# Encoder layer with a mixture of experts: the routing chain rewritten, the closing sums and scaling in halves and on three engines, the fifth weight tile issued behind the first row gather

## The reference

```python
x = x + y @ w_out
h = rmsnorm(x, ffn_norm)
# group top-1 of 4, then expert top-2 of the 8 in that group
lg = h @ w_group + b_group;  grp = argmax(lg);  p_grp = softmax(lg)[grp]
le = (h @ w_router + b_router)[grp];  top_p, top_i = top_k(softmax(le), 2)
gate = p_grp * top_p / sum(top_p);  expert = grp * 8 + top_i
# for each token and each of its two experts (w_gate, w_up 2048x768, w_down 768x2048)
x += gate * ((silu(h @ w_gate[e]) * (h @ w_up[e])) @ w_down[e])
return rmsnorm(x, final_norm)
```

## Time and profile before

| | |
|---|---|
| median of 3 runs | 2051.66 us (2050.88 to 2051.67) |
| the profiled execution | 2052.39 us, span 2050.5 us |
| TensorE busy | 1879.7 us, 92% of the span |
| VectorE busy | 584.6 us, 29% |
| ScalarE, GpSimd busy | 174.1 us, 241.6 us |
| moved by DMA | 681.13 MB, mean 332 GB/s |

### The profile page before, as it was taken

One profiled execution on the slowest core, in us unless ns is written; L12 is line 12 of the kernel. 1 busy time (PEld: TensorE's weight loads), 2 busy tenths in 40 slices (PEclk: granted clock), 3 DMA queues, 4 the chain that ended last, 5 costly groups with the idle time before them and its releaser, 6 DMA issues.

```text
span 2050.5 us, 21069 instructions
## 1 busy us (share of the span) xinstructions
PE 1879.7 (92%) x9592; PEld 1072.9 (52%) x9592; DVE 584.6 (29%) x789; ACT 174.1 (8%) x248; POOL 241.6 (12%) x92
## 2 busy tenths in 40 slices
PE   8999999999949999999988989998898999889895
PEld 6887878788834444344444434444443444434342
DVE  3221656611141222221222222122222222222224
ACT  4000110100110000100000010000001000000102
POOL 3323444433300000000000000000000000000000
PEclk9999999999969999999999999999999999999998
DMA  7222132443269999999999999999999999999993
GB/s 271 82 78 82 62 103 87 164 176 114 105 271 389 432 431 429 429 429 429 431 427 430 430 430 430 429 430 428 429 430 429 429 431 427 432 429 428 430 429 136
DMA packets 67131, 681.13 MB, mean 332 GB/s; under 512 B 10272, under 2 KB 13536, under 8 KB 40288
## 3 DMA queue, kind: packets, MB, share of 16 engines
q1 hardware_dynamic: 63632, 670.11, 78.4%
q0 software_dynamic: 2304, 8.39, 1.0%
q10 hardware_dynamic: 1104, 1.25, 0.2%
HBM read 679.73 MB, written 8.39 MB: 336 GB/s over the span
## 4 chain that ended last, share of the span: by engine, by line
PE 58%; DMA 38%; DVE 3%; POOL 0%; issue 0%; ACT 0%; SPq 0%; DVEq 0%; POOLq 0%
DMA region_rest<-in_w_gate 23%; PE banks L982 21%; PE banks L690 14%; PE banks L871 9%; DMA region_h<-in_w_gate 6%; DMA region_w<-in_w_gate 6%; PE banks L1001 5%; PE banks L973 4%; DMA region_rest<-in_w_down 2%; PE banks L960 1%; PE banks L949 1%; PE banks L908 1%; PE banks L755 1%; PE banks L767 1%; DMA region_h<-x_rows,region_rest 1%; DVE region_rest L1196 0%
## 5 line engine op out<-in xcount | busy, mean ns | idle before, releaser
L982 PE MATMUL banks<-region_rest,region_w 128*64 128x384 f32 x2432 | 411.5, 492 | 49.9 <-DMA region_rest<-in_w_gate 33.3
L982 PEld LDWEIGHTS banks<-region_rest,region_w 128*64 128x64 f32 x2432 | 175.9, 138 | 277.1 <-issue 199.0
L1428 DVE TENSOR_TENSOR region_x<-banks,region_x 128x1024 f32<-128x1024 f32 x128 | 150.8, 1219 | 585.7 <-PE banks L973 585.7
L690 PE MATMUL banks<-split_h,split_w 128*128 128x512 f32 x896 | 286.0, 396 | 3.6 <-POOL split_w L437 3.1
L1001 PE MATMUL banks<-region_rest,region_w 128*64 128x512 f32 x936 | 232.9, 655 | 19.5 <-DVE region_w L1453 13.0
L437 POOL TENSOR_TENSOR split_w<-region_rest,split_w 128x2048 fp32r<-128x2048 f32 x43 | 201.4, 4684 | 319.5 <-DVE split_w L1086 319.5
L690 PEld LDWEIGHTS banks<-split_h,split_w 128*128 128x128 f32 x896 | 169.0, 189 | 40.2 <-issue 4.9
L690 PE MATMUL banks<-split_w 128*128 128x512 f32 x448 | 175.0, 391 | 0.0
L483 POOL DMA_INDIRECT region_h<-x_rows,region_rest x16 | 16.0, 1000 | 1281.1 <-PE banks L960 1263.5
L871 PE MATMUL banks<-split_w,split_h 128*128 128x512 f32 x512 | 160.1, 394 | 0.0
L982 PE MATMUL banks<-region_h,region_w 128*64 128x384 f32 x832 | 142.9, 497 | 17.4 <-DMA region_h<-in_w_gate 10.1
(11 more groups left out here) (196 smaller groups left out, 1159.2 us busy)
## 6 DMA issues: line engine op xcount, KB each, us to landing
region_rest<-in_w_gate SPq DMA_DIRECT2D x40, 3072.0 KB, 31.6
region_rest<-in_w_down SPq DMA_DIRECT2D x39, 3072.0 KB, 31.0
region_rest<-in_w_up SPq DMA_DIRECT2D x36, 3072.0 KB, 29.9
region_h<-in_w_up SPq DMA_DIRECT2D x14, 3072.0 KB, 30.0
region_w<-in_w_up SPq DMA_DIRECT2D x14, 3072.0 KB, 29.4
region_w<-in_w_down SPq DMA_DIRECT2D x13, 3072.0 KB, 31.1
region_h<-in_w_gate SPq DMA_DIRECT2D x12, 3072.0 KB, 31.1
region_w<-in_w_gate SPq DMA_DIRECT2D x12, 3072.0 KB, 31.1
```

Source lines behind the costliest of these rows:

```text
L690: mm = t_.matmul(ps[:, 4 * (c % 2) + m, :], w[s][:, kk, cols_m], h[:, k, :], start=(k == 0 and w is w_hi and h is h_hi), stop=(k == KT - 1 ...
L982: mm = t_.matmul(ps[h * SLOTS:(h + 1) * SLOTS, u, 0:HF], hTe[:, k, :], ring_gu[slot][:, kk, h * HF:(h + 1) * HF], start=(k == 0), stop=(k ...
L1428: v.tensor_tensor(tile, ps[:, 2 + 2 * c:4 + 2 * c, :], tile, ALU.add).then_inc(comb_added, 1)
```

## The change

- **Routing.** The logits are no longer multiplied by 1/rms. In its place the bias is multiplied by rms and added before the last part of the logits arrives; the exponentials take 1/rms as their scale, one for each of 4 blocks. The sum over earlier blocks and the base of each expert's slots come out of TensorE (4 products in place of 1 for the rank, one of them issued before the routing is known; 4 small ones for the counts behind them). VectorE makes the slots in 4 operations; `compare` for the first pair comes in two halves of 512 columns, and `plan` starts on the first half. The overflow slots are made later, behind `read_plan`.
- **Rows into `hTe`.** Transposes are signalled after 8 and after 16, `store_rows_T` takes two operations of 512 columns, parts 0 and 1 wait for a half each.
- **Tile 4** waits for the first gather too (`rows_gathered`).
- **Last tile** (part 5 of the last expert) is issued as 3 DMAs of a third each, `down` waits for each third.
- **End.** `combine` for c = 0 waits only for the first half of the low parts. VectorE scales columns 0 to 1407; for the other 640 POOL multiplies by `final_norm` into `gained`, and ScalarE, behind its last root, by 1/rms. The output of t waits for both.
- One small constant (`e64_next`) is made by POOL in the first stage.

```diff
@@ sync
             sp.wait_ge(x2_sq, 4 * NT)
+            sp.wait_ge(rows_gathered, 16)
             tile(4)
...
-                tile(n)
+                if n == TILES - 1:
+                    for k in range(DK):
+                        sp.dma_start(ring_down[slot_of(n)][:, k:k + 1, :], wdn_v[E - 1, 1][:, k:k + 1, :])\
+                            .then_inc(last_landed[k], 16)
+                else:
+                    tile(n)
...
                 sp.wait_ge(out_ready, t + 1)
+                sp.wait_ge(out_rest_ready, t + 1)
@@ gpsimd
+            pool.wait_ge(final_landed, 16)
+            for t in range(NT):
+                pool.wait_ge(comb_added, 4 * E - 6 + 2 * t)
+                g.tensor_tensor(gained[:, t, :], x_sb[:, t, FINAL:], final_row[:, FINAL:], ALU.mult).then_inc(f_gained, 1)
@@ scalar
+            ae.wait_ge(x2_rms, 3)
             ae.wait_ge(exp_in, 1)
-            a.activation(lgm, lgm, ACT.Exp).then_inc(exp_out, 1)
+            for t in range(NT):
+                a.activation(lgm[:, t, :], lgm[:, t, :], ACT.Exp, scale=stat[:, 20 + t:21 + t]).then_inc(exp_out, 1)
...
+            for t in range(NT):
+                ae.wait_ge(f_gained, t + 1)
+                ae.wait_ge(f_rinv, t + 1)
+                a.activation(x_sb[:, t, FINAL:], gained[:, t, :], ACT.Copy, scale=stat[:, 8 + t:9 + t]).then_inc(out_rest_ready, 1)
@@ tensor
+            t_.matmul(by_tile, ones[0:1, :], e64[0:1, :]..., start=True, stop=False)
             pe.wait_ge(routed, 1)
-            t_.matmul(ps[:, 0, 0:NT * E], before, A..., start=True, stop=True)
-            t_.matmul(ps[:, 1, 0:NT * E], ones, A..., start=True, stop=True).then_inc(counted, 1)
+            for n in range(1, NT):
+                t_.matmul(ps[:, 6, n * E:NT * E], ones, flat[:, 0:(NT - n) * E], start=False, stop=False)
+            t_.matmul(ps[:, 6, 0:NT * E], before, flat, start=False, stop=True).then_inc(counted, 1)
+            for t in range(NT):
+                mm = t_.matmul(ps[:, 7, 0:E], ones, A[:, t, :], start=(t == 0), stop=(t == NT - 1))
+            mm.then_inc(counted, 1)
...
                 if t == 0:
-                    pe.wait_ge(m_lo_ready, i * 4 + 4)
                     pe.wait_ge(back_ready, i * 2 + 2)
                 for c in (0, 1):
+                    if t == 0:
+                        pe.wait_ge(m_lo_ready, i * 4 + (3 + c))
...
-                pe.wait_ge(hte_ready, e + 1)
                 for part in range(4):
+                    if part < 2:
+                        pe.wait_ge(hte_ready, 2 * e + part + 1)
@@ vector
-                v.scalar_tensor_tensor(x_sb[:, t, :], x_sb[:, t, :], stat[:, 8 + t:9 + t], final_row,
+                v.scalar_tensor_tensor(x_sb[:, t, 0:FINAL], x_sb[:, t, 0:FINAL], stat[:, 8 + t:9 + t], final_row[:, 0:FINAL],
```

More of the change, by code:

```diff
@@ L57 @@
 NOBODY = 4096
+FAR = 8192.0
 UK = 4
@@ L244, in build @@
         tile_landed = [sem(f"tile_landed{s}") for s in range(RING + 1)]
+        last_landed = [sem(f"last_landed{k}") for k in range(DK)]
         over_landed = [sem(f"over_landed{s}") for s in range(PARTS)]
@@ L993, in transpose_act, with down @@
                 pe.wait_ge(at_ready, e + 1)
-            def down(b, part, slot):
+            def down(b, part, slot, pieces=None):
                 q = part - 4
                 for kk in range(DK):
+                    if pieces:
+                        pe.wait_ge(pieces[kk], 16)
                     for n in (0, 1):
@@ L1009, in landed @@
                 return s
-            plan(0)
+            plan(0, True)
             pe.wait_ge(plan_read, 9)
@@ L1032, in _ @@
                     pe.wait_ge(m_lo_ready, 2 * e)
-                for part in (4, 5):
-                    down(b, part, landed(n + part))
+                down(b, 4, landed(n + 4))
+                if e < E - 1:
+                    down(b, 5, landed(n + 5))
+                else:
+                    down(b, 5, slot_of(n + 5), last_landed)
             for t in range(NT):
@@ new lines, in _, with per_choice @@
+            next_first = e64_next.rearrange("p (a b) -> p a b", a=1).to_broadcast([P, NT, E])
+            then(v.tensor_tensor(t1, rank, next_first, ALU.is_ge))
+            then(v.scalar_tensor_tensor(Q, t1, FAR, rank, ALU.mult, ALU.add))
+            def per_choice(of):
+                return of.rearrange("p (k a) b -> p k a b", k=1).to_broadcast([P, 2, NT, E])
+            then(v.tensor_tensor(both, full, per_choice(Q), ALU.mult))
+            then(v.tensor_reduce(slot.rearrange("p a k -> p k a"), both, AX.X, ALU.add))
@@ L1400, in next_compare, with compare @@
+            def compare(first, last, ready, order=0):
+                n = last - first
+                v.tensor_tensor(pick[:, first:last], row_slot[order].rearrange("p (a b) -> p a b", a=1).to_broadcast([P, n, P]),
+                                slot.rearrange("p a (b c) -> p (a b) c", c=1)[:, first:last].to_broadcast([P, n, P]),
+                                ALU.is_equal).then_inc(ready, 1)
             def next_compare(i, order=0):
@@ L1404, in next_compare @@
                 ve.wait_ge(slots_shifted, i)
-                compare(order)
+                compare(0, NA, pick_ready, order)
             def read_plan(i, s):
```

114 lines of the change are left out of this document (64 added, 50 removed).

## The result

The changed kernel takes 2039.97 us (median of 4 runs, 2038.62 to 2043.66), the kernel before took 2051.27 us beside it (4 runs, 2050.46 to 2051.67): ratio 0.9941, interval 0.9929 to 0.9953. It is faster; the forecast was 2040.0.

The account below looks back on a forecast made before the run. The weight stream through DMA was taken to set the loop's pace, leaving its start and its end. 8.8 us at the start and 3.05 at the end, 11.85, gave 2040 us for the median; range for 8 in 10, 2035.5 to 2044.5.

Parts of the forecast that it names:

- (a) to (c): Routing, from the group's maximum through counts to `compare`: shorter work starts `plan` and issues the first gather 4.7 us earlier.
- (d): First gather: without tile 4 the queue empties 7.3 us earlier, so it lands at 599.6, 7.6 us earlier.
- (e): Start of `gate_up`: behind 8 transposes and 512 columns, at 601.35 for 610.59; 0.4 allowed for half clock; tile 6 8.8 earlier.
- (f): Held tile 4: through at about 608.5, before part 4 needs it; costs nothing, and the last tile lands 8.8 us earlier.
- (g): Last tile in thirds: TensorE's 1.75 us wait ahead of part 5 is gone, and no more.
- (h): `combine` c = 0 at the end: starts behind the first low half, 1.25 us earlier.
- (i): TensorE's clock in `combine`: a shorter gap may keep it up, worth 1.4 us; at an even chance, 0.7.
- (j): ScalarE's scalings behind the last root: the first output goes out 0.65 us later against the sums.
- (k): VectorE's closing scaling shrinks from 2.35 to 1.65 us but buys nothing; POOL's multiplications, 1.9 us, run beside the sums.
- The rival of a constant time from issue to landing: First gather takes as long as before wherever the queue ends, landing 602.5 to 606.3; 2043 to 2047 us; chance 0.15.
- the one of a head start given back: Expert loop: TensorE, not DMA, holds the stream, only the end's 3 us remain; 2048 to 2050 us; chance 0.04.
- The one in which the gather goes ahead of tile 5: First gather at the page's price without the queue, landing 595 to 598; 2035.5 to 2038.5 us; chance 0.12.

Follow-up runs that it names:

- a1: The changed kernel with tile 4 issued at once, not held behind the first gather; 2044.1 us, ratio 0.995.
- a2: The kernel before with one line added, so that tile 4 waits for the first gather; 2044.14 us, ratio 0.9954.
- a7: The changed kernel with store_rows_T in one operation of 1024 columns again and one signal behind all 16 transposes; 2039.56 us in one run.
- a4: The changed kernel with the last tile in one DMA again instead of thirds; 2043.57 us in one run.
- a6: The changed kernel with the closing scaling on VectorE alone, 2048 columns at a time; 2040.53 us in one run.
- d1: The changed kernel with tile 5 too issued behind the first gather; 2038.83 us, ratio 0.9929.
- a5: The changed kernel with combine waiting for both low halves again; 2044.51 us in one run.
- a3: The changed kernel with the end of the kernel before: last tile whole, combine behind both low halves, scaling on VectorE alone; 2044.71 us, ratio 0.9949.
- after: The first profiled execution of the changed kernel itself, against the kernel before; 2043.66 us.
- c1: The changed kernel with POOL's last product held until VectorE's first scaling is done; 2039.16 us in one run.
- b2: The changed kernel with the first output block scaled by VectorE alone in two halves, each stored at once, POOL's last product held until then; 2040.07 us, ratio 0.993.
- b3: The changed kernel with first (in two halves, each stored at once) and last output blocks scaled by VectorE alone, POOL and ScalarE only on blocks 1 and 2; 2039.22 us.

## Why the prediction was right, step by step

- **(a) to (c)** forecast `plan` and the gather 4.7 us earlier; they are 5.0 and 4.9 earlier. The counting products that VectorE waits for take 2.09 us (1.49 and 0.60), not 2.4.
- **(d)** forecast the landing 7.6 earlier, measured 7.4. But the reason given was only half right, and that the number fits is in part luck. It reads the landing as the queue's end. a1 has the gather landing 2.7 us ahead of tile 4, and a2 has 4.60 us for it as the queue runs out. In the changed kernel weights, tile 5 among them, lay in the queue when it was issued, the queue was through some 7 us later (594.44 to about 601.7, 361 GB/s in the window to 602), and it took 9.08. In a2 it was issued as the queue ran out and took its own 4.60, so both land at 24 to 25. The price of the Trainium skill that I had as a rival ("DMA: Bandwidth & Descriptors", section "Anatomy of one DMA": an estimate of 4.4 us) looks right where the engines are free, 4.60 and 4.2 us, but by chance: it is for 1 MB, and 43 rows are 0.35 MB, for which the same section gives an estimate of 2.8 us. Beside weights, with 9.1 to 15.4 us, it does not hold at all.
- **(e)** forecast `gate_up` 9.2 earlier; measured 8.8. I had let it start behind 8 transposes; TensorE does all 16 in order (1.99), so the halves save VectorE's 1.24 and the gaps, 1.4 us by a7, and not the transposes. The 0.4 allowed for more half clock in part 0 was not lost in this trace (6.78 us from `gate_up` to tile 6, 7.20 before), but elsewhere it was, up to 8.1 us (a4, a6). Tile 6 went out 9.3 earlier, within a scatter of 2 us from trace to trace, forecast 8.8.
- **(f)** tile 4 lands at 36.3, 12 us behind its issue, long before part 4 (at 53.4); DMA idles for 1.3 us ahead of tile 6. The stream keeps 8.9 us, the last tile 8.8, the forecast's 8.8. That the agreement is so close is luck: by the nine traces with this start it is 6.6 to 8.9 at the last tile. d1 shows the limit: 4.3 us more at tile 6's issue, with tile 5 moved behind the gather, are worth nothing.
- **The loop** is as it was.
- **(g)** was put too low, 1.75 and "no more": 2.07. The wait of 1.74 is gone, the 48 products in one piece take 10.54 us instead of twice 5.37, and part 4 starts 0.1 earlier against the last landing. In the profiled execution 0.39 of it is seen, for part 3 was half-clocked.
- **(h)** 1.25 forecast, 1.16 measured.
- **(i)** the clock does what the step says: where it stays up the sums take 1.76 us less than before, in the profiled execution and three more of the ten traces with the short gap. In the other six, with 12.0 to 12.3, it is 0.6 to 0.9. The reason given, the shorter gap, is not borne out: a5 keeps the clock with the long one. The even chance was about right, and that it came out in the profiled execution is luck.
- **(j)** 0.65 forecast (its own terms, 2037.19 and 0.74 against 2037.31, give 0.62, and 640 columns at the price of 512 are 0.78), 1.03 measured: the sums end sooner, ScalarE does not keep up with them, and its last sum of squares begins 0.52 us behind the last sum (2026.87 against 2026.35), where it was 0.18. **(k)** "buys nothing" is right. POOL's products take 1.53 to 1.58 us, not 1.9, and run beside the sums at no cost as forecast, all but the last one, which costs VectorE's first scaling 1.2 us.
- **The sum at the end**: 3.05 forecast, 3.66 in the profiled execution, 4.45 in the one taken again, counted from the last tile's landing and against the kernel before. Part of that is the one trace of the kernel before: a2 and a3 have the same end and need 36.8 and 36.6 us for it where it needs 37.8. Against them the changed kernel gains 2.5 to 3.5.
- **The whole**: 2039.97 against 2040.0 is closer than the steps are, since (e), (g), (i) and (j) are each off by 0.3 us or more and the changed kernel's medians in two places are 2 us apart (2039.97 and 2042.1). The mechanism, that the stream keeps what tile 6 gains, is shown.

The rival of a constant time from issue to landing fell with a1 and a2 (13.36 and 4.60), the one of a head start given back with the stream's 8.9 us, the slower one with the loop's rows. The one in which the gather goes ahead of tile 5 was wrong for this kernel: it took 9.08 us beside tile 5's weights.

## What to carry to other kernels

Ask of each transfer on the critical path what lies in the queues when it is issued: here one line that keeps a tile of 3 MB out of the way until a gather has landed, a tile not needed for 30 us more, gave 6.7 of the stream's 8.9 us, and made most of the shorter routing worthless at the landing (0.4 us instead of 3.2). Count packets there and not bytes: beside weights a gather of 29 rows took only 2 us less than one of 105. Two edits that shorten the same wait are not added up but tried alone and together. And an earlier start of the consumer is worth nothing if the stream's own bytes are moved back for it (d1).

## What the runs showed of the hardware

- VectorE and POOL: one VectorE operation with two inputs in SBUF (1.69 us alone) takes 2.86 to 3.06 us when POOL's product of two SBUF tensors (1.53 us) runs in its time, and ends 1.48 to 1.49 us behind it (after, c1, b2). The Trainium skill's page "SBUF — State Buffer", section "Who interferes with whom", has this: an instruction of VectorE with two SBUF inputs contends with one of GpSimd that reads SBUF, and the port pair that they share is an exclusive lock. The traces agree, 1.2 to 1.4 us for a product of 1.53. The page lets the one that issues first win; the traces of c1 and b2 have VectorE starting 0.04 to 0.05 us ahead and losing, which is less than the starts can be trusted.
- The same first gather (43 rows, 144 packets) took 4.2, 4.6, 9.1, 11.6 and 13.4 us from issue to landing, by what was queued ahead of and beside it. Beside a full queue the 15 others of the kernel before, of 29 to 105 rows, took 12.9 to 15.4.
- A packet of 16 KB of instructions, 1.0 to 1.4 us long, that falls among the last outputs goes with one DMA engine being through 0.3 to 1.4 us behind the other 15 (before, a2, a3, a6, b3).
- The last 3 MB tiles do not come at full speed: the windows of the changed kernel fall from 432 GB/s to 262, 203 and 190 in the 12 us ahead of 2006. The busy share falls with the rate: GB/s over share is 422 to 430 in all four rows, so the engines that are busy run at their speed and others have run out. The four outputs of 1 MB land 2.5 us apart, that is full speed. Why the engines end so far apart was not tried.

```profile
1990.00:1994.00 4.00, 2.08 (x14) 0.77 (x12) 0.19 (x1) 0.00 (x0) 0.00 (x0) 1.00 1.02 432
1994.00:1998.00 4.00, 4.00 (x16) 1.59 (x14) 0.00 (x0) 0.00 (x0) 0.00 (x0) 0.57 0.61 262
1998.00:2002.00 4.00, 2.75 (x17) 1.14 (x13) 1.02 (x2) 0.00 (x0) 0.00 (x0) 1.00 0.48 203
2002.00:2006.00 4.00, 3.79 (x18) 1.35 (x20) 0.15 (x1) 0.00 (x0) 0.00 (x0) 1.00 0.45 190
```
